# Ten expert units a layer, places in the order of the experts' counts, and router work moved, in a two-layer encoder

## The reference, cut to what matters

```python
def _moe(h, router_w, w_gate, w_up, w_down):
    probs = jax.nn.softmax((x @ router_w).astype(jnp.float32), axis=-1)
    top_v, top_i = lax.top_k(probs.reshape(T, N_GROUPS, EXPERTS_PER_GROUP), TOP_K)
    g_sel = jnp.argmax(jnp.sum(top_v, axis=-1), axis=-1)
    ...
    def expert_block(args):
        xblk, e = args
        hid = jax.nn.silu(xblk @ w_gate[e]) * (xblk @ w_up[e])
        return hid @ w_down[e]
    ...
def reference(...):
    for layer in range(DEPTH):
        ...  # y = mixer(h)
        h = _layer_norm(DN_ALPHA * h + y, ln_w[layer, 0], ln_b[layer, 0])
        y = _moe(h, router_w, moe_w_gate[layer], moe_w_up[layer], moe_w_down[layer])
        h = _layer_norm(DN_ALPHA * h + y, ln_w[layer, 1], ln_b[layer, 1])
```

## Time and profile before

| | us |
|---|---|
| median of 3 runs | 1387.13 (1386.0 to 1387.42) |
| the profiled execution | 1386.77 |
| its span | 1384.9 |
| MoE units of layer 0, from gate of unit 0 to the end of the last down | 296.9 to 574.8 |
| the same of layer 1, from gate of unit 0 to the start of the last down | 1081.7 to 1350.1 |

### The profile page before, as it was taken

How to read it: one execution, slowest core, us unless ns; L and a number is a source line. 1 busy time by engine, 2 the same in 40 slices (tenths; PEclk the granted TensorE clock), 3 DMA queues, 4 the chain that set the end, 5 groups by cost and what they waited for, 6 DMA issues and landing times.

```text
span 1384.9 us, 16143 instructions
## 1 busy us (share of the span) xinstructions
PE 1335.2 (96%) x6723; PEld 604.2 (44%) x6723; DVE 528.3 (38%) x1008; ACT 189.8 (14%) x319; POOL 167.2 (12%) x126
## 2 busy tenths in 40 slices
PE   8999999989999999999999999999898899999996
PEld 4444464533333333344555555555545333333332
DVE  1344762453111111430365666665636221111117
ACT  0025400100000000011111111111111000000000
POOL 0000400041000000200122332222300500000011
PEclk9999989999999999999999999999999999999998
DMA  9920065188999997643321122200094789999943
GB/s 352 370 74 1 31 273 212 53 318 312 410 420 406 422 405 290 247 116 111 90 61 37 25 61 61 61 0 0 4 390 182 294 327 426 402 427 407 426 178 150
DMA packets 83993, 305.84 MB, mean 221 GB/s; under 512 B 6516, under 2 KB 50904, under 8 KB 71512
## 3 DMA queue, kind: packets, MB, share of 16 engines
q1 hardware_dynamic: 61872, 264.65, 49.0%
q10 hardware_dynamic: 17448, 23.46, 4.7%
q0 software_dynamic: 4608, 16.78, 3.2%
HBM read 271.31 MB, written 33.55 MB: 220 GB/s over the span
## 4 chain that ended last, share of the span: by engine, by line
PE 86%; DVE 9%; DMA 1%; issue 1%; ACT 1%; POOL 0%; DVEq 0%; POOLq 0%; SPq 0%
PE ps L596 24%; PE ps L759 14%; PE ps L631 12%; PE ps L475 8%; PE ps L553 7%; PE ps L746 4%; PE ps L781 4%; PE ps L811 2%; PE ps L581 2%; PE ps L545 1%; DVE S L1590 1%; PE ps L534 1%; PE ps L619 1%; PE ps L799 1%; PE ps L521 1%
## 5 line engine op out<-in xcount | busy, mean ns | idle before, releaser
L596 PE MATMUL ps<-W,S 128*32 128x512 f32 (+1 forms) x2048 | 338.5, 600 | 2.2 <-DVE S L1513 2.2
L759 PE MATMUL ps<-hT,W 128*128 128x512 f32 x512 | 232.6, 593 | 0.7 <-ACT W L890 0.7
L596 PE MATMUL ps<-S 128*64 128x512 f32 (+1 forms) x512 | 224.8, 597 | 0.4 <-DVE S L1513 0.4
L631 PE MATMUL ps<-W,hT 128*32 128x512 f32 (+1 forms) x1024 | 171.5, 601 | 1.0 <-DVE hT L1527 1.0
L596 PEld LDWEIGHTS ps<-W,S 128*32 128x32 f32 (+1 forms) x2048 | 97.6, 114 | 150.1 <-issue 145.8
L759 PEld LDWEIGHTS ps<-hT,W 128*128 128x128 f32 x512 | 92.9, 191 | 90.3 <-issue 88.4
L631 PE MATMUL ps<-S,hT 128*32 128x512 f32 (+1 forms) x256 | 113.0, 594 | 1.0 <-DVE hT L1527 1.0
L890 ACT ACTIVATE hT<-ps 128x512 f32<-128x512 f32 x74 | 42.3, 598 | 376.7 <-PE ps L631 287.0
L596 PEld LDWEIGHTS ps<-S 128*64 128x64 f32 (+1 forms) x512 | 62.1, 124 | 71.8 <-issue 70.5
L1721 POOL TENSOR_TENSOR W<-S,sq 128x256 f32<-128x256 f32 x64 | 73.5, 1149 | 160.9 <-PE ps L781 117.3
L475 PE MATMUL ps<-W,hT 128*128 128x512 f32 x192 | 85.5, 604 | 2.1 <-DMA W<-w_in_even 2.1
(11 more groups left out here) (246 smaller groups left out, 1346.7 us busy)
## 6 DMA issues: line engine op xcount, KB each, us to landing
W<-moe_w_gate SPq DMA_DIRECT2D x24, 2048.0 KB, 12.3
W<-moe_w_up SPq DMA_DIRECT2D x24, 2048.0 KB, 13.1
W<-moe_w_down SPq DMA_DIRECT2D x24, 2048.0 KB, 11.4
S<-moe_w_gate SPq DMA_DIRECT2D x8, 2048.0 KB, 13.5
S<-moe_w_up SPq DMA_DIRECT2D x8, 2048.0 KB, 13.8
S<-moe_w_down SPq DMA_DIRECT2D x8, 2048.0 KB, 16.7
W<-w_in_odd SPq DMA_DIRECT2D x32, 512.0 KB, 6.3
slot_rows<-S ACTq DMA_DIRECT2D x4, 2816.0 KB, 20.0
```

Of the source, the lines that this page charges most:

```text
L596: last = pe.matmul(ps[a:a + n, bank, :], xgT[:, c, a:a + n], w[L][slot_of(e)][:, c, :], start=(c == 0), stop=(c == ND - 1))
L631: last = pe.matmul(ps[a:a + n, 2 + half, :], hidT[:, c, a:a + n], wd[L][slot_of(e)][:, c, half * 512:(half + 1) * 512], start=(c == 0), st ...
L759: last = pe.matmul(ps[:, f % 2, :], ring[slot][:, f, c, :], hT[:, c, :], start=(c == 0), stop=(c == ND - 1))
```

## The change

Constants: 32-slot strips; STRIPS gives the strips of 16 places, 3, 3, 2 four times and then 2 four times: 40 strips, ten units. A place is filled by rank. Experts 0, 1 and 2 keep the first three places (the favour in `c_iota` ranks 0 and 1 first and 2 last); the others are ranked by count, and the first eight ranks get the 96-slot places, the rest the 64-slot ones. The order is computed on DVE and read by SP into registers, so that weights are loaded in that order.

```diff
+STRIP = 32
+STRIPS = [3, 3, 2] * 4 + [2] * 4
+FIRST_STRIP = [sum(STRIPS[:p]) for p in range(NE)]
+NU = sum(STRIPS) * STRIP // P
+CAP, SMALL = 3 * STRIP, 2 * STRIP
+BY_RANK = [p for p in range(NE) if STRIPS[p] == 3] + [p for p in range(3, NE) if STRIPS[p] == 2] + [2]
+WIDE = STRIPS.count(3)
+MAXX = 12
-ROUNDS = 2
+ROUNDS = 3
+    favour = -np.arange(NE)
+    favour[0:3] += [2 * int(BIG), int(BIG), -int(BIG)]
...
+        def places_of(u):
+            return sorted({p for p in range(NE) if 4 * u < FIRST_STRIP[p] + STRIPS[p] and FIRST_STRIP[p] < 4 * u + 4})
+        def slot_of(p):
+            return p % 3
+        def final_unit(p):
+            return (FIRST_STRIP[p] + STRIPS[p] - 1) // 4
```

SP's loads. The wait on `table_done` and the register loads are new:

```diff
                 for k in (1, 2):
                     load_rows(L, k, k)
+                sp.wait_ge(table_done, 2 * L + 1)
+                expert_at = {}
                 for u in range(NU):
                     if 1 <= u < NU - 2:
                         sp.wait_ge(xgT_ps[L], u * 2)
                         load_rows(L, u + 2, (u + 2) % 3)
+                    freed = [p for p in range(3, NE) if final_unit(p - 3) == u]
+                    for p in freed:
+                        at = T_ORDER + BY_RANK.index(p)
+                        expert_at[p] = sp.value_load(tbl[0:1, at:at + 1], min_val=0, max_val=NE - 1)
+                    if freed:
+                        sp.wait_ge(gate_mm[L], u + 1)
+                    for p in freed:
+                        load_gate(L, expert_at[p], slot_of(p))
+                    if freed:
+                        sp.wait_ge(up_mm[L], u + 1)
+                    for p in freed:
+                        load_up(L, expert_at[p], slot_of(p))
+                    freed = [p for p in range(3, NE) if final_unit(p - 3) == u - 1]
+                    if freed:
+                        sp.wait_ge(down_mm[L], 2 * u)
+                    for p in freed:
+                        load_down(L, expert_at[p], slot_of(p))
```

Routing on DVE. The centring of tile 3 moves behind the selections of tiles 0 to 2; a ranking stands before the slots and the order table after them:

```diff
                     if t == NT - 1:
+                        centre(2 * L, t)
                         shift(t)
...
+                done(v.scalar_tensor_tensor(r_key, r_cnt, float(NE), favour, ALU.mult, ALU.add))
+                done(v.tensor_tensor(table, other, mine, ALU.is_gt))
+                done(v.tensor_reduce(r_rank, table, AX.X, ALU.add))
+                v.tensor_scalar(r_cap, r_rank, float(WIDE), float(CAP - SMALL), ALU.is_lt, ALU.mult)
+                done(v.tensor_tensor(table, mine, places, ALU.is_equal))
+                done(v.tensor_tensor(table, table, pairs_of(r_rank, base_by_rank)[1], ALU.mult))
+                done(v.tensor_reduce(r_base, table, AX.X, ALU.add))
+                done(v.scalar_tensor_tensor(r_key, r_cnt, -float(SMALL), r_cap, ALU.add, ALU.subtract))
...
+                v.tensor_tensor(r_key, r_cap, r_base, ALU.add)
...
                 ins.then_inc(slots_done, 1)
+                done(v.tensor_tensor(by_rank, view(r_rank[0:1], 0, [[0, NE], [1, NE]]),
+                                     view(iota[0:1], 0, [[1, NE], [0, NE]]), ALU.is_equal))
+                done(v.tensor_tensor(by_rank, by_rank, view(iota[0:1], 0, [[0, NE], [1, NE]]), ALU.mult))
+                done(v.tensor_reduce(r_ord[0:1], by_rank, AX.X, ALU.add))
+                v.tensor_copy(tbl[0:1, T_ORDER:T_ORDER + NE], r_ord[0:1]).then_inc(table_done, 1)
```

The start of the MoE. TensorE's selection matmuls go tile by tile with both halves, and up of unit 0 waits for the slots (it overwrites the PSUM bank that the routing reads). ACT, not DVE, copies the second half of the first rows and their transposes:

```diff
-                for half in range(2):
-                    for t in range(NT):
-                        pe.wait_ge(sel_done, L * NT + t + 1)
+                for t in range(NT):
+                    pe.wait_ge(sel_done, L * NT + t + 1)
+                    for half in range(2):
...
                     gate(u)
+                    if u == 0:
+                        pe.wait_ge(slots_done, L + 1)
                     up(u)
...
+                act.wait_ge(side_ps, 3 * L + 2)
+                copy(first_rows[:, 512:1024], ps[:, 3, :]).then_inc(side_copied, 1)
+                for half in range(2):
+                    act.wait_ge(xgT_ps[L], half + 1)
+                    copy(xgT[:, half * 4:half * 4 + 4, :],
+                         ps[:, 4 + half, :].rearrange("p (c n) -> p c n", c=4)).then_inc(xgT_done[L], 1)
...
-                dve.wait_ge(side_ps, 3 * L + 2)
-                v.tensor_copy(first_rows[:, 512:1024], ps[:, 3, :]).then_inc(side_copied, 1)
-                copy_rows(0)
```

The last tile before the routing (both layers) is taken by halves: its first half is added, measured and transposed while the last output projection still runs, and the logits are cut to match (`last_logits`); in layer 1 ACT's scaling is split too. The router work of layer 0 moves from the input projections to the retention scores, on TensorE and DVE:

```diff
-            project(4)
-            router_sums(0, 3)
-            project(5)
-            router_spread(0, 3)
-            for n in (6, 7):
+            for n in range(4, 8):
                 project(n)
...
                     scores(hd + 1)
+                if hd == 0:
+                    router_sums(0, 7)
+                elif hd == 2:
+                    router_spread(0, 7)
...
-            turn_h(1, NT - 1)
-            logits(0, NT - 1)
+            last_logits(0)
```

More of the change, by code:

```diff
@@ L191, in encoder_kernel @@
         r_skip = r_(NE)
+        r_key, r_rank, r_base, r_cap, r_ord = (r_(NE) for _ in range(5))
         r_blk = r_gt[:, 0:MAXX * NE]
@@ L434, in turn_h @@
                 elif n % 2:
-                    pe.wait_ge((op_used, op_added)[n // 2], 2 * t + 2)
+                    pe.wait_ge((op_used, op_added)[n // 2], 2 * t + halves[-1] + 1)
                 else:
                     pe.wait_ge(ln_done, (n - 1) * NT + t + 1)
-                for half in range(2):
+                for half in halves:
                     for c in range(4):
@@ L722, in _ @@
                     logits(0, 1)
-                    logits(0, 2)
+                    turn_h(1, NT - 1, (0,))
+                    logits(0, 2, range(4))
                     out_project(k, mixT, w_out0, range(4, ND), False, True).then_inc(op_ps, 1)
@@ L871, in _ @@
                     logits(1, 1)
-                    logits(1, 2)
+                    turn_h(3, NT - 1, (0,))
+                    logits(1, 2, range(4))
                     out_project(k, OG, w_out1, range(4, HG), False, True).then_inc(op_ps, 1)
@@ L890, in copy, with turn_copies @@
                 return nc.scalar.activation(o, i, ACT.Copy)
-            def turn_copies(n, t):
-                for k in (2 * t, 2 * t + 1):
+            def turn_copies(n, t, halves=(0, 1)):
+                for k in (2 * t + half for half in halves):
                     act.wait_ge(hT_ps, n * 2 * NT + k + 1)
@@ L1114, in _, with scale_output @@
             act.wait_ge(rms_done, 1)
-            def scale_output(t):
-                for k in (2 * t, 2 * t + 1):
+            def scale_output(t, halves=(0, 1)):
+                for k in (2 * t + half for half in halves):
                     act.wait_ge(op_ps, 2 * NT + k + 1)
@@ L1132, in _ @@
             turn_copies(3, 2)
-            scale_output(3)
-            turn_copies(3, 3)
+            for half in range(2):
+                scale_output(3, (half,))
+                turn_copies(3, 3, (half,))
             norm_std(2, 3)
@@ L1303, in tile_of, with statistics @@
                 return halves, ps[:, 2 * t:2 * t + 2, :] if n % 2 else halves
-            def statistics(n, t):
+            def statistics(n, t, halves=(0, 1)):
                 _, src = tile_of(n, t)
-                for half in range(2):
+                for half in halves:
                     last = v.bn_stats(col("st", 6 * half, 6), src[:, half, :])
@@ L1348, in norm_mixer @@
                     shift(t)
-                add(3)
-                statistics(n, 3)
+                add(3, (0,))
+                v.bn_stats(col("st", 0, 6), h[:, 3, 0:512])
+                add(3, (1,))
+                statistics(n, 3, (1,))
                 for t in range(3):
                     scaled_logits(L, t)
-                centre(n, 3)
+                dve.wait_ge(std_done, n * NT + 4)
+                done(v.reciprocal(col("rst1", 3, 1), col("std", 3, 1)))
                 done(scaled_logits(L, 3))
@@ L1372, in add_mixer, with add @@
             def add_mixer(L):
-                def add(t):
-                    for half in range(2):
+                def add(t, halves=(0, 1)):
+                    for half in halves:
                         k = 2 * t + half
@@ L1441, in route, with pairs_of @@
                                            first_sel[:, t, :], ALU.is_equal, ALU.add).then_inc(sel_done, 1)
-                done(v.tensor_scalar(r_nbk, r_cnt, float(CAP), None, ALU.is_gt))
+                def pairs_of(a, b):
+                    return (view(a, 0, [[1, NE], [0, NE]]), view(b, 0, [[0, NE], [1, NE]]))
+                favour, base_by_rank = (iota[:, P + EPG * EPG + n * NE:P + EPG * EPG + (n + 1) * NE] for n in range(2))
+                table = r_gt.rearrange("p (e r) -> p e r", r=NE)
@@ L1454, in route @@
+                done(v.tensor_tensor(r_skip, r_skip, r_key, ALU.subtract))
+                v.tensor_tensor(by_token(r_d), per_expert(r_base), ranks, ALU.add)
                 done(v.tensor_tensor(by_token(r_over), by_token(r_over), view(r_skip, 0, [[0, NT], [1, NE]]), ALU.mult))
```

150 lines of the change are left out of this document (65 added, 85 removed).

## The result

The changed kernel takes 1343.59 us (median of 4 runs, 1340.68 to 1345.17), the kernel before 1386.57 us beside it (1385.63 to 1387.42): ratio 0.9687, 95% interval [0.9671, 0.9702]. It is faster, as forecast, but by 43.0 us where 63 were forecast, and 2.6 us above the top of the range. The profiled execution took 1340.68 us (span 1338.8) against 1386.77 (span 1384.9): 46.1 us of gain against 62.7. These 16.6 us are what follows explains; 2.9 us more lie between that execution and the median.

The account below looks back on a forecast made before the run. TensorE bounds the kernel before; the DMA was to bound the changed one. Down of the last but one unit starting 34.6 and 35.1 us earlier (69.7), less 5 and 2, gave 62.7 off: 1324 us, range 1309 to 1341.

Parts of the forecast that it names:

- Sign and mechanism: MoE units: faster, chance 0.95; two units less save TensorE 91.2 us, but DMA becomes the bound from about unit 4.
- The stream: Expert loads, SP's resumption to down of unit 8: 86.5 MB at 426 GB/s, 203.1 us, plus 3.8 us fixed.
- 2.5 for gaps and clock: Deduction per layer: 1 us for gaps while the stream fills, 1.5 us for TensorE's clock.
- fixed 3.8 us: Expert loads: the part of a lone transfer's 8.7 us landing time beyond 4.9 us for its bytes.
- the 2.6 us of added routing: DVE's routing before the scatter in layer 1: SP resumes 2.6 us later, net of earlier logits.
- Rival B: Expert loads: queue runs dry between bursts, mean 412 GB/s, 6.9 us more a layer plus clock, 1342 us; chance 0.12.
- rival C: Expert loads: a full queue runs slowly at 366 GB/s, 33 us more a layer, 1390 us; chance 0.03.
- Start of unit 1, rows, router: Unit 1 waits some 5 us for rows, begins within 1 us of before; layer 0's router move costs -1 to +1.
- The tails: Behind the start of down of unit 8: same work, except 2 us lost in layer 1 to the last store.
- Behind it the work is the same: After down of unit 8 starts: last down's weights land at +15.7, and it starts at +16.6 us, as before.
- such a 1.8: TensorE's clock: each of four stalls a layer may bring 1.8 us, mostly absorbed; 1.5 us a layer deducted with this.
- The range: 8 in 10, whole kernel: 1309 to 1341 us, from DMA rates up to 440 GB/s, scatter timing and the stop-and-go case.

Follow-up runs that it names:

- half_weights: The changed kernel loading only half of each gate, up and down matrix from the fourth place on (products not the reference's): 1306.19 us.
- twelve_units: The changed kernel with 96 slots for all 16 places, so twelve units, everything else of the change kept: 1386.24 us.
- router_back: The changed kernel with layer 0's router work put back between the input projections: 1343.69 us.
- before_tail_late: The kernel before, with norm loads (and w_v1 in layer 0) held until down of unit 10 is done, as in the changed kernel: 1401.49 us.
- last_down_moved: The changed kernel with place 15's down matrix issued early into place 13's gate space, and w_v1 after the second tile's gathers: 1330.50 us; repeated, 1331.06 us.
- down_three_quarters: The changed kernel loading three of four chunks of each down matrix from place 3 on (products not the reference's): 1313.80 us.
- v1_late: The changed kernel with layer 0's load of w_v1 issued only after all gathers of that layer have landed: 1338.80 us.
- norms_behind: last_down_moved with the two norm loads of each layer also waiting for the first tile's gathers: 1332.73 us.

## Why the prediction was right and wrong

**Sign and mechanism: right.** The DMA takes over as the bound from the middle of the layer on, TensorE waits for up weights and for the down of the fourteenth place, and two units of TensorE's work give half of what they are worth. By the profiled executions, 91.2 us are removed, 14.7 and 11.5 are lost to the stream (down of unit 8 against TensorE alone: 518.52 - 503.8, and 45.6 - 34.1), 18.9 to the tails: 46.1. By `half_weights` the stream's own parts are 12.1 and 13.9, together nearly the same; TensorE alone is 2.6 us later in layer 0 and 2.3 earlier in layer 1 than the forecast put it, and what makes that was not looked into.

**The stream: right.** In layer 0, SP was forecast at 307.9 and resumed at 309.26: the CAST of the slots starts at 294.07, 3.4 us later than before (290.65), where 2.9 was forecast, and from there to SP it took 15.2 us where it took 14.3 before (290.65 to 304.97). From there down of unit 8 was 206.9 us away by the bytes and 2.5 for gaps and clock: 209.4. It took 209.3 in layer 0 (309.26 to 518.52) and 210.7 in layer 1 (1069.17 to 1279.82). After the fixed 3.8 us and before the start, 86.5 MB moved at 421 GB/s; 426 less the gaps is the same thing (the DMA share from 309.3 to 518.5 us is 1.00). In layer 1, from the v-projection to SP it took 498.4 us, where it took 498.5 before: the 2.6 us of added routing that the forecast had there did not show, and that made up for a stream 1.3 us over its sum. This is luck, and why it did not show is open. Rival B's 412 and rival C's 366 are out. The Trainium skill's rule ("SBUF — State Buffer", "Summary: rules for kernel authors": some 358 GB/s end to end) stays contradicted for a lone core: this kernel holds 427 to 429 GB/s in its full windows.

**Start of unit 1, rows, router: right.** Gate of unit 1 begins at 315.39 where it began at 314.56, behind a wait of 4.4 us for the rows; forecast 5 us and within 1. `twelve_units` and `router_back` show the rest to be nothing.

**The tails: wrong.** The step that failed is "Behind it the work is the same. The last down needs the weights of place 15, issued when down of unit 8 ends (+7.0), into a queue that has emptied by then". Its words on the last down are right (it starts 18.2 us after the other, at 536.74, with 1.8 of that by the clock and a wait of 1.0 for its weights), but I followed only that matrix to its consumer, not the 5.2 MB that stand behind it in SP's order (1 MB in layer 1), and not what they run beside. With twelve units they were issued 14 us earlier relative to the last store, because the load in front of them waited for an earlier product. The price was taken as 0 in layer 0 and as 2 us in layer 1 (the store, 2.62 us with an empty queue); measured are 11.3 and 7.6. `before_tail_late` shows that the order alone does it, with 11.0 us in the kernel before, and `last_down_moved` that it goes away in layer 0 once the last matrix is early and w_v1 late (41.2).
Another 3.5 of the 18.9 us are the clock: down of unit 8 starts after a stall and takes 8.80 us in place of 7.02, in both layers. I had counted such a 1.8 for each of four stalls a layer, "most of it absorbed"; this one is not, for nothing behind it is bound by the DMA. That leaves 4.4. The stores account for 3.8 of them: 9.86 and 9.82 us against 7.80 and 8.05 in `before_tail_late`, where the last down matrix isn't issued with them. That this matrix is the reason is argued, not shown by a run of its own; the stores of 7.91 and 8.02 beside half of it, and 9.10 and 8.41 beside three quarters, agree.

In terms of the sum: start of down in layer 0 1.2 us later than forecast with its deductions (518.52 against 514.8 + 2.5), tail +11.3, layer 1's stretch 1.5 us better (-34.1 against -32.6), its tail 7.6 against 2: 1.2 + 11.3 - 1.5 + 5.6 = 16.6 us.

**The range.** It had been made of the DMA's rate and the scatter, and both ends priced the stream. Nothing in it stood for the stretch behind the stream, which had the value "the same" and no bounds.

What is open: the 1.8 us of clock weren't tested by themselves (only in `half_weights` and `down_three_quarters`, where the stall is gone, they are gone too), and no version was tried that brings layer 1's tail back to its 51.4 us without giving it back at the gathers.

## What to carry to other kernels

When fewer iterations of a loop cover the same loads, follow every load to the one in front of it on its queue, past the loop's end too: a prefetch that waits for the last product also holds back what stands behind it, and it then lands on the store and the gathers that nothing covers. Give the last weights a space that is free earlier, and ask of each byte moved out of one stretch which stretch it is moved into. A step that is taken as "the same as before" needs bounds like any other.

## What the hardware showed

- A store of 0.5 MB on ACT's queue takes 2.6 us with nothing else under way. As the last store beside loads of SP's queue it takes 4.0 to 9.9 us, also when those were issued 14 us ahead of it (6.8 us in layer 0 before). The packets of the changed kernel show two parts in this. From 528 to 532 us only SP's queue moves data, though the store was issued at 527.97; from 533 to 535 both do (packets, MB, share of 16 engines; q1 holds SP's loads, q10 ACT's stores):

```profile
q1 hardware_dynamic: 77, 1.26, 93.1%
...
q1 hardware_dynamic: 32, 0.52, 72.5%
q10 hardware_dynamic: 35, 0.14, 17.4%
```

  First comes a wait: no packet of the store moves for 4.3 us. Then the two queues alternate, 32 packets to 35; but a packet of the down matrix has 16 KB and one of the store 4 KB, so the store gets a fifth of the bytes. In layer 0 before, the first packet comes after 3.5 us, and then, from 561 to 563 us, there are 104 packets of w_v1 to 100 of the store, all of 4 KB. With an empty queue (layer 1 before), and in the repeat of `last_down_moved` with 0.5 MB of the loads left, the first comes after 0.8 us. It isn't a queue behind all that was issued, which would be 17 us for 7.3 MB; what sets the wait of 3.5 to 4.6 us beside a longer backlog, no run here shows. The Trainium skill says that each engine takes turns between its queue rows, one packet at a time ("DMA: Bandwidth & Descriptors", "Queues, rings and completion order"). The counts of 32 to 35 and 104 to 100 agree, as far as the profile's packets are those of the page; the wait ahead of them isn't explained by it.
- This core holds 427 to 429 GB/s, at a share of 1.01, through whole stretches of 23 to 25 us; 421 over 205 us with its gaps.
- A stall of 3 us ahead of a product can cost 1.8 us more in it: the 32 matmul records of down took 8.80 us in place of 7.02. After stalls of 1.1 and 1.4 us the same product took 7.10 (layer 1 of `v1_late` and `last_down_moved`), after 3.6 and 3.9 us 10.02 (layer 1 of `norms_behind` and `router_back`), and after 3.5 us in layer 0 of `router_back` only 8.52.
- The changed kernel's four runs lie 4.5 us apart. Those of the kernel before lie 1.8 apart beside them, but 9.1 among the 13 beside the first experiments, so a few us between two single executions can be spread.
